# Layer 0's rotary products on GpSimd instead of VectorE in a two-layer hybrid decoder kernel

## The reference

```python
def apply_rope(x, cos, sin):
    xf = x.astype(jnp.float32)
    x1, x2 = jnp.split(xf, 2, axis=-1)
    return jnp.concatenate([x1 * cos - x2 * sin, x2 * cos + x1 * sin], axis=-1).astype(x.dtype)
...
aq = apply_rope(rms_norm(aq.reshape(b, s, A_HEADS, HEAD_DIM), a_q_norm_g[j]), cos, sin)
ak = apply_rope(rms_norm(ak.reshape(b, s, A_KV_HEADS, HEAD_DIM), a_k_norm_g[j]), cos, sin)
iq = apply_rope(iq.reshape(b, s, IDX_HEADS, IDX_DIM), cos_i, sin_i)
ik = apply_rope(ik[:, :, None, :], cos_i, sin_i)[:, :, 0, :]
```

## Time and profile before

| | |
|---|---|
| median of 3 executions | 2528.34 us (2523.71 to 2530.15) |
| the profiled execution's own time | 2531.02 us |
| its span, first to last instruction | 2529.3 us |
| TensorE busy | 2431.7 us, 96% |
| VectorE busy | 1614.6 us, 64% |
| ScalarE busy | 1059.8 us, 42% |
| GpSimd busy | 1290.7 us, 51% |
| mean granted TensorE clock | 0.984 |

### The profile page before, as it was taken

One profiled execution on the slowest core, in us unless ns is written; L12 is line 12 of the kernel. 1 busy time (PEld: TensorE's weight loads), 2 busy tenths in 40 slices (PEclk: granted clock), 3 DMA queues, 4 the chain that ended last, 5 costly groups with the idle time before them and its releaser, 6 DMA issues. The chain is left out here.

```text
span 2529.3 us, 31058 instructions
## 1 busy us (share of the span) xinstructions
PE 2431.7 (96%) x11073; PEld 1940.9 (77%) x11073; DVE 1614.6 (64%) x2338; ACT 1059.8 (42%) x1821; POOL 1290.7 (51%) x676
## 2 busy tenths in 40 slices
PE   8889998999999999999999999979999999999999
PEld 6778875557888888888888877857687888888887
DVE  6878878988875654465448656675556544564483
ACT  4556887656645232223222356254442322232210
POOL 3212325888862664576459222164336654665490
PEclk9999998999999999999999999979999999999999
DMA  5311131004001211221111231230112111211121
GB/s 159 88 46 42 44 86 47 1 17 133 18 18 51 67 34 34 65 66 50 33 50 59 75 96 38 72 108 13 51 34 67 51 33 49 66 58 34 40 67 67
DMA packets 165306, 140.88 MB, mean 56 GB/s; under 512 B 24457, under 2 KB 136146, under 8 KB 165202
## 3 DMA queue, kind: packets, MB, share of 16 engines
q1 hardware_dynamic: 158738, 132.98, 17.7%
q10 hardware_dynamic: 6464, 6.56, 0.9%
HBM read 116.17 MB, written 13.63 MB: 51 GB/s over the span
## 5 line engine op out<-in xcount | busy, mean ns | idle before, releaser
L2496 PE MATMUL ps<-h_hi,w_hi 128*128 128x512 f32 x1672 | 661.0, 395 | 0.0
L2498 PE MATMUL ps<-h_hi,w_lo 128*128 128x512 f32 x1672 | 653.1, 391 | 0.0
L2497 PE MATMUL ps<-h_lo,w_hi 128*128 128x512 f32 x1672 | 653.0, 391 | 0.0
L830 POOL TENSOR_TENSOR w_lo<-w_raw,w_hi 128x1024 fp32r<-128x1024 f32 x69 | 184.2, 2669 | 357.6 <-ACT w_hi L1453 354.0
L2498 PEld LDWEIGHTS ps<-h_hi,w_lo 128*128 128x128 f32 x1672 | 315.1, 188 | 66.6
L2497 PEld LDWEIGHTS ps<-h_lo,w_hi 128*128 128x128 f32 x1672 | 315.3, 189 | 65.2 <-issue 1.9
L2496 PEld LDWEIGHTS ps<-h_hi,w_hi 128*128 128x128 f32 x1672 | 315.1, 188 | 65.4 <-issue 2.4
L2380 DVE TENSOR_TENSOR x_res<-ps,x_res 128x1024 f32<-128x1024 f32 x224 | 268.6, 1220 | 115.5 <-PE ps L2498 115.5
L848 POOL TENSOR_TENSOR w_lo<-w_raw,w_hi 128x1024 fp32r<-128x1024 f32 x112 | 267.5, 2404 | 127.2 <-ACT w_hi L1315 89.9
L2361 DVE TENSOR_TENSOR u_all<-ps,u_all 128x512 f32<-128x512 f32 x112 | 77.0, 690 | 381.1 <-ACT u_all L1326 381.1
L2496 PE MATMUL ps<-w_hi,uo_hi 128*128 128x512 f32 x784 | 307.9, 393 | 5.9 <-DVE shared L2380 3.6
(11 more groups left out here) (382 smaller groups left out, 4453.7 us busy)
## 6 DMA issues: line engine op xcount, KB each, us to landing
w_raw<-in_mlp_w_up SPq DMA_DIRECT2D x64, 512.0 KB, 4.0
w_raw<-in_mlp_w_down SPq DMA_DIRECT2D x64, 512.0 KB, 3.6
w_raw<-in_even_w_in SPq DMA_DIRECT2D x23, 512.0 KB, 4.0
x_res<-in_x SPq DMA_DIRECT2D x16, 512.0 KB, 7.9
t<-xg SPq DMA_DIRECT2D x120, 64.0 KB, 2.0
w_raw<-in_odd_w_in SPq DMA_DIRECT2D x10, 512.0 KB, 3.9
scr_x<-x_res SPq DMA_DIRECT2D x8, 512.0 KB, 2.6
x_res<-scr_x SPq DMA_DIRECT2D x8, 512.0 KB, 4.9
```

The source lines that it names most:

```text
L830: g.tensor_tensor(w_lo[:, k, :], w_raw[:, n % 2, :], w_hi[:, k, :].bitcast(F32), ALU.subtract).then_inc(w_ready, 1)
L2496: t_.matmul(out_, ah, bh, start=first, stop=False)
L2497: t_.matmul(out_, ah, bl, start=False, stop=False)
L2498: return t_.matmul(out_, al, bh, start=False, stop=last)
```

## The change

In layer 0 GpSimd takes both products of every rotation, in place in the same two buffers, and VectorE keeps the sum (and the keys' reciprocal and scaling). GpSimd waits for the swapped halves, for the tables before the first rotation, and for the transposes of the indexer's key before rotations 8 and 9; it raises `rot_read`, for which VectorE waits as before. The products stand in GpSimd's queue ahead of splits: rotations 0 to 3 ahead of the split of unit 4, rotations 4, 5 and 6 ahead of the splits of units 5, 6 and 7, then two rotations ahead of each split of units 8 to 12 (7 and 8, and so on to 15 and 16), and 17 to 19 ahead of that of unit 13. Layer 1's rotations stay on VectorE.

```diff
+            def rotation_products(r):
+                kind, j, hf = ROPE0[r]
+                b, tk = r % 2, slice(hf * HT, (hf + 1) * HT)
+                pool.wait_ge(half_moved[b], 64 * (r // 2 + 1))
+                if r == 0:
+                    pool.wait_ge(tables_ready, 2)
+                if kind == "ik":
+                    pool.wait_ge(iw_turned, hf + 1)
+                g.tensor_tensor(xg[:, b, :], xg[:, b, :], cosT[:, tk], ALU.mult)
+                g.tensor_tensor(t2[:, b, :], t2[:, b, :], sinT[:, tk], ALU.mult).then_inc(rot_read, 1)
+
+            ROTATED = {4: range(4), 5: (4,), 6: (5,), 7: (6,)}
+            ROTATED.update({n: (2 * n - 9, 2 * n - 8) for n in range(8, 13)})
+            ROTATED[13] = (17, 18, 19)
             for n in range(U_OUT0 + 2):
+                for r in ROTATED.get(n, ()):
+                    rotation_products(r)
                 if 4 <= n < U_OUT0:
                     split_low(n)
...
-                dve.wait_ge(half_moved[b], 64 * (r // 2 + 1))
-                if kind == "ik":
-                    dve.wait_ge(iw_turned, hf + 1)
-                v.tensor_tensor(t2[:, b, :], t2[:, b, :], sinT[:, tk], ALU.mult).then_inc(rot_read, 1)
-                link(v.tensor_tensor(xg[:, b, :], xg[:, b, :], cosT[:, tk], ALU.mult))
+                if layer == 1:
+                    dve.wait_ge(half_moved[b], 64 * (r // 2 + 1))
+                    v.tensor_tensor(t2[:, b, :], t2[:, b, :], sinT[:, tk], ALU.mult).then_inc(rot_read, 1)
+                    link(v.tensor_tensor(xg[:, b, :], xg[:, b, :], cosT[:, tk], ALU.mult))
                 dve.wait_ge(rot_read, r + 1)
```

## The result

The median of 5 executions is 2541.42 us (2537.95 to 2541.73), that of the kernel before, measured beside it, 2527.12. The ratio is 1.0047 with a 95% interval of 1.0035 to 1.0059: slower by 11.9 us (8.8 to 14.9). The two medians by themselves lie 14.3 us apart, inside that interval. The forecast was 2547 us, slower, within 2531 to 2560.

The account below looks back on a forecast made before the run. TensorE, busy for 2431.7 of 2529.3 us, was taken to bound the kernel, VectorE counting only where TensorE waits. Terms 12 + 6 + 1 = 19 us gave 2547 us against the median; 8 in 10 range 2531 to 2560.

Parts of the forecast that it names:

- Up to the first scores: Layer 0's early rotation chain: products and splits on GpSimd delay VectorE's sums and copies; TensorE loses 12 us.
- walk of four queues: Rotations up to the first scores, four queues timed side by side: transposes at 93.0 us, 10.6 us later; first score added 116.3.
- During the scores: Rotations 11 to 19: about 2.03 of 2.54 us hit busy VectorE, less 1.33 removed; 0.7 us each, 6 us in all.
- Rival 1: Score stage: VectorE is relieved, GpSimd's pieces falling into its idle fifth; 10 us faster, 2518 us; chance 0.06.
- The clock: TensorE's granted clock falls behind a gap of 2 us; one such dip more than before expected, 1 us.
- The price of a product: One GpSimd product of 128x512 float32 takes 1.27 us, 2.54 us a rotation; low end 1.09, high end 1.48.
- What costs nothing: Loads behind later splits, SyncE's DMAs and the search after rotation 19, which starts later by as much as TensorE is late.
- Unit 4's split: GpSimd's split behind the first products: the exception among the later splits that cost nothing, at most 0.3 us.
- Rival 2: It evens out: the early chain loses little and the scores gain as much; within 0.3%, 2531 us; chance 0.14.
- Rival 3: Milder than worked out: chain delay 5 us, scores cost 6; 2540 us; chance 0.2, within the forecast's sign.
- the signs looked for: Products near 1.27 us, GpSimd busy some 50 us more, transposes' gap near 12 us, first score 10 us later, 2 us adds.

Follow-up runs that it names:

- early_only: Changed kernel with GpSimd taking only the products of rotations 0 to 10, VectorE keeping those of 11 to 19; 1.0038 against the kernel before, 9.6 us slower.
- narrow: Changed kernel with each product cut to 32 of its 512 columns, the other 480 left out; 0.9940 against the kernel before, 15.2 us faster.
- the two runs beside the kernel before: Kernel before, whole; GpSimd additionally multiplies tables into an unread spare tile (1.0085, 21.5 us slower) or fills it with six memsets instead (1.0013, 3.3 us).
- after_all_later: Changed kernel, small instructions moved: nine one by one ahead of rotations 11 to 19, eighteen ahead of the MLP; 1.0036 against the kernel before, 9.1 us.
- before_ends_later: Kernel before with only eighteen small instructions moved ahead of the MLP, the first part staying in front of rotation 6; 0.9996, 1.0 us faster.
- scores_only: Kernel before with GpSimd taking the products of rotations 11 to 19 only; 1.0005, 1.3 us, within what can be told from no change.
- rot_ahead: Changed kernel with products 6 and 7 put ahead of the splits of units 6 and 7 in GpSimd's queue; 1.0057 against the kernel before.
- beside_products: Kernel before, whole, with GpSimd also multiplying the tables into an unread spare tile in the places of the change; 1.0085, 21.5 us slower.

## Why the prediction was right, and where it was not

Of the sum, 12 + 6 + 1 = 19 us, the traces give 10.2, 0.5 and nothing; the forecast held because its largest term did.

**Up to the first scores (12 us): right.** The walk of four queues held step by step. On the time axis of before (after's plus 2.03) sum 5 ends at 82.8 us (forecast 83.0), sum 6 starts at 90.3 (91.7), the transposes at 91.8 (93.0), the first score added at 113.0 (116.3). The key is late by 9.4 (10.6) and the first score by 10.2 (12). The cause is the one named. early_only shows that the loss lies on this chain, narrow that it comes with the products' length and not with the order, the waits or the hand-over, and the two runs beside the kernel before that GpSimd's reading alone can do it: there the key is 11.7 us late, with memsets 0.7. Of the 9.4 us the small instructions carry 3.2 (after_all_later); the rest is the longer products and the sums held behind products and splits, which no run parts. One reading was too wide: not all small instructions stand beside GpSimd, the two reciprocals of one input pass in 0.18 us. What came short is the walk behind sum 6, where the splits of units 8 and 9 started at 101.3 and 110.2, earlier than 102.6 (2.4 before its end at 105.0) and 112.0.

**During the scores (6 us): mis-sized, it was 0.5.** The step that failed is "of 2.54 us of products about 2.03 hit it while it has work". VectorE's busy time in the stage rose by 1.1 us while 13.7 us of products left it, so its waiting grew by 14.8 us, 1.5 for each of the ten rotations there: about the 1.33 removed, and not 2.03. Part of the overlap is paid by GpSimd, whose products wait in their turn (1516 ns on the mean for those with the sines). And "they come on top of the splits, which stay" was too much: the sums lost 4.4 us of waiting that the splits had laid on them. Rival 1's own point of decision, 1.33 us in each 2.54, is about where the chip came out.

**The clock (1 us): nothing.** Before, three stretches of 4 us had a granted clock of 0.59 or 0.60: the one of the earlier trace rows, behind a gap of 2.13 us, and these two in the score stage, behind gaps of 2.02 and 2.05 us; 3 x 1.6 = 4.8 us.

```profile
132.00:136.00 4.00, 4.00 (x14) 3.40 (x15) 2.44 (x6) 1.43 (x4) 0.00 (x0) 0.60 0.09 25
...
156.00:160.00 4.00, 4.00 (x15) 3.34 (x16) 2.14 (x5) 1.53 (x4) 0.00 (x0) 0.59 0.46 126
```

After, the score stage has no gap over 1.6 us and no such stretch, but the two long gaps ahead of it cost nearly as much. The stretches around those, after (columns as in the earlier trace rows):

```profile
88.00:92.00 4.00, 2.26 (x8) 1.98 (x9) 3.52 (x17) 1.53 (x4) 0.00 (x0) 0.50 0.13 33
92.00:96.00 4.00, 4.00 (x17) 3.29 (x16) 0.92 (x6) 2.38 (x4) 2.02 (x2) 0.88 0.22 54
...
108.00:112.00 4.00, 4.00 (x12) 3.42 (x12) 3.80 (x2) 1.21 (x3) 3.94 (x3) 0.50 0.60 150
112.00:116.00 4.00, 4.00 (x18) 3.38 (x17) 3.56 (x5) 1.97 (x4) 1.54 (x2) 0.82 0.12 36
```

0.50 is the lower of the two levels, 1.2 GHz: (2.26 + 4.00) x 0.50 + 4.00 x 0.12 + 4.00 x 0.18 = 4.3 us. "Behind a gap of 2 us the granted clock falls" did not hold in every trace: in before_ends_later it stayed at 1.00 behind two gaps of 2.02 us (at 100.68 and 127.83), and in scores_only the stretch from 180 to 184 us had 0.69 behind one of 1.38 us.

**The price of a product (1.27 us): right**, as the pieces that met nothing took 1.26 to 1.30. The lower estimate of 1.12 us from the Trainium skill ("GPSIMD Engine Reference", section "Elementwise — side-by-side cycle accounting"), with its sum of 14, comes nearer to 11.9, but by accident: no product took so little, and what was too high is the score stage.

**What costs nothing.** "After rotation 19 VectorE's search of levels starts later by as much as TensorE is late" held: of 10.7 us at the end of the scores 9.9 remain at the end of the search. Unit 4's split, "at most 0.3 us", cost TensorE one wait of 0.37. That nothing is hidden in the search is truer than I used: three of my runs put small instructions into it, and it took 7 to 8 us longer in each.

**The rivals.** Rival 2 (evens out) is what happened in the score stage alone. Rival 3 (5 us for the chain and 6 for the scores, 2540) has the nearest total with the sizes the wrong way round. Of the signs looked for, the gap before the transposes (10.6 us for near 12), GpSimd's busy time (58.9 us more, over 50 expected, since products wait too) and the late first score came; adds of 2 us were the exception, the mean is 0.966.

## What to carry to other kernels

Handing a two-input product from VectorE to an idle GpSimd relieves VectorE only by what GpSimd's reading does not take from it: here, in the score stage, 13.7 us went and 14.8 us of waiting came. Where the receiving stage is a chain of small dependent steps, look for the four-column instructions in it first: each that GpSimd's reading can hold may stand for a whole GpSimd instruction, and the chain pays that many times over. And before work is moved into a stage because its engine waits there for another, put something into that stage and see whether the wait shrinks.

## What the runs showed that I had not expected

- With a sixteenth of the reading, the same hand-over is worth 15.2 us (narrow); I had given the relief of VectorE 10 us at the most.
- With GpSimd busy back to back, VectorE's four-column instructions, 0.16 us alone, got through at about one for each GpSimd instruction (the reciprocals, which were not held, left out), and starting GpSimd's work earlier changed nothing (rot_ahead).
- The length of a gap does not tell by itself whether TensorE's granted clock falls behind it: 1.87 us left it alone in before and 2.02 us twice in before_ends_later, 2.02 and 2.05 us in before were followed by 4 us at 0.60 and 0.59, and 1.38 us in scores_only by 4 us at 0.69. What else decides is open.
- From the start of the attention to the last transposition of `o_sum`, gains of 4.3 us (before_ends_later) and 13.4 us (narrow) shrank to 1.0 and 10.2. But a loss grew there as well, from 16.0 to 19.2 us (beside_products), and others stayed: 7.1 and 7.2 (after_all_later), 7.9 and 8.0 (early_only). So it is not gains that are taken; the stretch takes 349.4 to 351.3 us in seven of the fourteen traces and 352.9 to 355.3 in the others, and whether that goes by kernel or by execution is open.
